# Stick-breaking attention in a two-layer decoder trunk: sigmoids and one reverse running product in place of the log-space chain, the mask added on TensorE, the short query block first, and the four heads as one pipeline

## The reference

```
def stick_breaking_attention(q, k, v):
    """o_t = sum_{s<t} beta_ts prod_{s<j<t}(1-beta_tj) v_s, beta_ts = sigmoid(q_t.k_s/sqrt(d)).
    q, k, v: (B, L, H, Dh)."""
    ...
    def block(start):
        qb = lax.dynamic_slice_in_dim(q, start, Q_BLOCK, axis=1)
        z = jnp.einsum("bqhd,bkhd->bhqk", qb, k, preferred_element_type=jnp.float32) * scale
        causal = key_pos[None, :] < (start + jnp.arange(Q_BLOCK))[:, None]
        log_1m = jnp.where(causal, jax.nn.log_sigmoid(-z), 0.0)
        csum = jnp.cumsum(log_1m, axis=-1)
        log_w = jax.nn.log_sigmoid(z) + (csum[..., -1:] - csum)
        w = jnp.where(causal, jnp.exp(log_w), 0.0)
        return jnp.einsum("bhqk,bkhd->bqhd", w.astype(v.dtype), v)
```

## Time and profile before

| | us |
|---|---|
| median of three executions | 3452.55 |
| lowest and highest | 3443.03, 3460.74 |
| span of the profiled execution | 3441.6 |
| PE busy, weight loads busy | 2945.9 (86%), 2782.7 (81%) |
| DVE busy | 1343.9 (39%) |
| POOL busy | 944.0 (27%) |
| ACT busy | 746.9 (22%) |
| mean granted TensorE clock | 0.922 of full speed |

### The profile page before, as it was taken

How to read it: one execution, slowest core, us unless ns; L and a number is a source line. 1 busy time by engine, 2 the same in 40 slices (tenths; PEclk the granted TensorE clock), 3 DMA queues, 4 the chain that set the end, 5 groups by cost and what they waited for, 6 DMA issues and landing times.

```text
span 3441.6 us, 45325 instructions
## 1 busy us (share of the span) xinstructions
PE 2945.9 (86%) x17797; PEld 2782.7 (81%) x17797; DVE 1343.9 (39%) x2281; ACT 746.9 (22%) x1270; POOL 944.0 (27%) x390
## 2 busy tenths in 40 slices
PE   3999978776668899999999987755997999999996
PEld 2999966664448799999999986645996999999995
DVE  2664055544571544443434234063025332233223
ACT  3321133434562320000000033112033000000002
POOL 2344200000003333333434330400531544354430
PEclk8999988987778999999999998877998999999998
DMA  4222510000102211111122213686111211111101
GB/s 154 75 98 92 114 44 25 25 25 19 37 19 70 87 57 63 63 63 63 66 71 85 87 46 75 139 193 158 62 58 58 83 49 49 37 49 49 49 25 66
DMA packets 175482, 236.23 MB, mean 69 GB/s; under 512 B 56480, under 2 KB 140960, under 8 KB 173088
## 3 DMA queue, kind: packets, MB, share of 16 engines
q1 hardware_dynamic: 66064, 133.42, 13.0%
q10 hardware_dynamic: 109328, 101.54, 9.8%
HBM read 172.37 MB, written 62.55 MB: 68 GB/s over the span
## 4 chain that ended last, share of the span: by engine, by line
issue 34%; PE 32%; POOL 11%; DVE 9%; DMA 6%; ACT 5%; ACTq 2%; SPq 1%; POOLq 0%; DVEq 0%
POOL w_hi L554 7%; PE psum L582 7%; PE psum L583 6%; PE psum L584 6%; POOL w_lo L558 3%; DMA stage<-wstream 3%; PE psum L636 3%; DVE area L1701 2%; PE psum L825 2%; PE psum L817 1%; DVE area L2036 1%; PE psum L936 1%; DVE area L1706 1%; DMA area<-xT 1%; PE psum L833 1%
## 5 line engine op out<-in xcount | busy, mean ns | idle before, releaser
L582 PE MATMUL psum<-x_hi,w_hi 128*128 128x344 f32 (+2 forms) x3600 | 1176.8, 327 | 56.9 <-DVE x_lo L1724 34.3
L583 PE MATMUL psum<-x_lo,w_hi 128*128 128x344 f32 (+2 forms) x3600 | 1170.1, 325 | 0.0
L584 PE MATMUL psum<-x_hi,w_lo 128*128 128x344 f32 (+2 forms) x3600 | 1165.3, 324 | 0.0
L554 POOL TENSOR_TENSOR w_hi<-stage,const 128x1024 fp32r<-128x1024 f32 x193 | 471.8, 2445 | 2386.9 <-PE psum L584 2365.6
L582 PEld LDWEIGHTS psum<-x_hi,w_hi 128*128 128x128 f32 x3600 | 690.8, 192 | 62.3 <-DVE x_lo L1724 32.7
L583 PEld LDWEIGHTS psum<-x_lo,w_hi 128*128 128x128 f32 x3600 | 689.8, 192 | 1.9
L584 PEld LDWEIGHTS psum<-x_hi,w_lo 128*128 128x128 f32 x3600 | 690.8, 192 | 0.0
L558 POOL TENSOR_TENSOR w_lo<-stage,w_hi 128x1024 fp32r<-128x1024 f32 x193 | 475.8, 2465 | 15.1
L582 PE MATMUL psum<-act_hi,w_hi 128*128 128x344 f32 (+1 forms) x1056 | 347.8, 329 | 36.9 <-DVE area L2081 29.3
L2068 DVE TENSOR_TENSOR area<-area,psum 128x352 f32<-128x352 f32 (+1 forms) x132 | 68.0, 515 | 723.7 <-ACT area L1475 723.7
L584 PE MATMUL psum<-act_hi,w_lo 128*128 128x344 f32 (+1 forms) x1056 | 342.1, 324 | 0.0
(11 more groups left out here) (214 smaller groups left out, 2571.8 us busy)
## 6 DMA issues: line engine op xcount, KB each, us to landing
stage<-wstream SPq DMA_DIRECT2D x193, 512.0 KB, 3.3
s_set<-area ACTq DMA_DIRECT2D x8, 1860.0 KB, 7.0
proj<-area ACTq DMA_DIRECT2D x28, 520.0 KB, 2.7
area<-proj ACTq DMA_DIRECT2D x40, 256.0 KB, 4.4
resid<-area ACTq DMA_DIRECT2D x6, 1376.0 KB, 6.0
area<-resid ACTq DMA_DIRECT2D x6, 1376.0 KB, 8.3
area<-proj ACTq DMA_DIRECT2D x12, 520.0 KB, 4.6
area<-xT ACTq DMA_DIRECT2D x4, 1376.0 KB, 8.3
```

What stands on the lines that cost most here:

```text
L554: pool.tensor_tensor(per_block(w_hi[:, slot, :]), per_block(stage[:, h, :]), all_ones, ALU.mult).then_inc(high_split, 1)
L582: mm(out[:, 0:n], w_hi[:, slot, wk], hi[:, xk, a:a + n], start=first, stop=False)
L583: mm(out[:, 0:n], w_hi[:, slot, wk], lo[:, xk, a:a + n], start=False, stop=False)
L584: return mm(out[:, 0:n], w_lo[:, slot, wk], hi[:, xk, a:a + n], start=False, stop=last)
```

## The change

The weight of a key is now sigmoid(z) times the product of sigmoid(-z) over the nearer keys. Per block ACT makes two sigmoids straight from the scores' banks (`sb_gates`), DVE one reverse running product and one multiplication (`sb_weights`). The mask is a second product on TensorE: the identity times a tile `neg` that holds -1e30 above and on the diagonal is added to the scores of the block's own keys, so that sigmoid(z) is 0 there and sigmoid(-z) is 1. The short query block (16 rows) comes first, so that block i > 0 sees 16 + 128 i keys. g counts the blocks of all four heads, and one unrolled pipeline of 36 steps runs over them; q, k, v, the transposed values and the turned weights have two buffers each. The loads of the first two heads are issued ahead of the last DeltaNet block's work on ACT, and a table set with the sigmoid is loaded after it.

```
 def sb_views(carve):
...
+    v = {"wt": [carve(BLOCKS * P * i, BLOCKS, P) for i in range(2)]}
+    at = 2 * BLOCKS * P
+    v["beta"] = [carve(at + T * i, T) for i in range(3)]
+    v["stay"] = [carve(at + T * (3 + i), T) for i in range(2)]
...
+    v["neg"] = carve(at + 2 * BLOCKS * P, P)
...
+            def sb_scores(g):
+
+                hd, i = divmod(g, BLOCKS)
+                q0, nq, nk = query_block(i)
...
+                if g > 1:
+                    pe.wait_ge(sk["beta"], g if i in (0, BLOCKS - 1) else g - 1)
                 for a in range(0, nk, 512):
                     m = min(512, nk - a)
...
+                    z = bank[2 * (i % 2) + a // 512]
+                    d = max(q0, a)
+                    last = mm(z[0:nq, 0:m], sv["q"][hd % 2][:, q0:q0 + nq], sv["k"][hd % 2][:, a:a + m],
+                              start=True, stop=d >= a + m)
+                    if d < a + m:
+                        last = mm(z[0:nq, d - a:m], ident[:, 0:nq], sv["neg"][:, d - q0:a + m - q0], start=False, stop=True)
                 last.then_inc(sk["z"], 1)
...
+            for g in range(HEADS * BLOCKS):
+                sb_turn(g)
+                if g + 2 < HEADS * BLOCKS:
+                    sb_scores(g + 2)
+                sb_out(g)
+                if g % BLOCKS == V_AT and g // BLOCKS < HEADS - 1:
+                    sb_values(g // BLOCKS + 1)
...
             act.wait_ge(dn["qkv_loaded1"], 48 * 5)
             act.wait_ge(dn["z_loaded1"], 16 * 5)
...
+            act.wait_ge(dn["out"], BLOCKS - 1 + 2)
+            load_head(0)
+            load_head(1)
+            dn_act_blocks(BLOCKS - 1, (BLOCKS - 1) // 2, 1, TAIL)
+
+
+            nc.scalar.preload_act_table_set("sigmoid_and_others")
             act.wait_ge(dn["out"], BLOCKS + 2)
...
+            def sb_gates(g):
+
+                i = g % BLOCKS
+                _, nq, nk = query_block(i)
+                z = psum[0:nq, 2 * (i % 2):2 * (i % 2) + (nk + 511) // 512, :].rearrange("p b c -> p (b c)")[:, 0:nk]
+                act.wait_ge(sk["z"], g + 1)
+                if g > 1:
+                    act.wait_ge(sk["w"], g - 1)
+                A(sv["stay"][g % 2][0:nq, 0:nk], z, ACT.Sigmoid, scale=-1.0).then_inc(sk["stay"], 1)
+                if g > 2:
+                    act.wait_ge(sk["w_t"], turn_group(g - 3) + HEAD_GROUPS[(g - 3) % BLOCKS])
+                A(sv["beta"][g % 3][0:nq, 0:nk], z, ACT.Sigmoid).then_inc(sk["beta"], 1)
...
+            for g in range(HEADS * BLOCKS):
+                sb_evac(g)
+                if g + 2 < HEADS * BLOCKS:
+                    sb_gates(g + 2)
+                    if (g + 2) % BLOCKS == BLOCKS - 1 and g // BLOCKS < HEADS - 2:
+                        load_head(g // BLOCKS + 2)
+                sb_high(g)
+                if g % BLOCKS == V_AT and g // BLOCKS < HEADS - 1:
+                    sb_value_evac(g // BLOCKS + 1)
...
+            def sb_weights(g):
+
+                _, nq, nk = query_block(g % BLOCKS)
+                stay, beta = sv["stay"][g % 2], sv["beta"][g % 3]
+                rev = stay[0:nq, nk - 1::-1] if nk == T else stay[0:nq, 0:nk][:, ::-1]
+                dve.wait_ge(sk["stay"], g + 1)
+                ch(V.tensor_tensor_scan(rev, rev, rev, 1.0, mul, ALU.min))
+                ch.sync()
+                dve.wait_ge(sk["beta"], g + 1)
+                V.tensor_tensor(beta[0:nq, 0:nk - 1], beta[0:nq, 0:nk - 1], stay[0:nq, 1:nk], mul).then_inc(sk["w"], 1)
...
+            sb_weights(0)
+            sb_weights(1)
+            for g in range(HEADS * BLOCKS):
+                if g + 2 < HEADS * BLOCKS:
+                    sb_weights(g + 2)
+                sb_low(g)
```

More of the change, by code:

```diff
@@ L101, with query_block, value_group, turn_group @@
 GROUPS_BEFORE = {"gates": 0, "in_proj": 6, "w_out_a": 90, "w_out_b": 96, "ssm_in": 114, "glu_a": 138, "glu_b": 150}
-WT_BEFORE = [sum((i + 4) // 4 for i in range(b)) for b in range(BLOCKS)]
-WT_GROUPS = 3 + sum((i + 4) // 4 for i in range(BLOCKS))
+def query_block(i):
+    q0 = TAIL + (i - 1) * P if i else 0
+    return q0, P if i else TAIL, q0 + (P if i else TAIL)
+V_AT = 4
+HEAD_GROUPS = [(i + 4) // 4 for i in range(BLOCKS)]
+def value_group(hd):
+    return 0 if hd == 0 else hd * 3 + (hd - 1) * sum(HEAD_GROUPS) + sum(HEAD_GROUPS[0:V_AT + 1])
+def turn_group(g):
+    hd, i = divmod(g, BLOCKS)
+    return 3 + hd * (3 + sum(HEAD_GROUPS)) + sum(HEAD_GROUPS[0:i]) + (3 if i > V_AT and hd < HEADS - 1 else 0)
 GATE_DVE = 3
@@ new lines, in sb_scores, with sb_turn @@
+                last.then_inc(sk["z"], 1)
+            def sb_turn(g):
+                _, nq, nk = query_block(g % BLOCKS)
+                pe.wait_ge(sk["w"], g + 1)
+                for n, j0 in enumerate(range(0, g % BLOCKS + 1, 4)):
+                    t = turn_group(g) + n
+                    pe.wait_ge(sk["wt_sb"], t - 1)
+                    for j in range(j0, min(j0 + 4, g % BLOCKS + 1)):
+                        w = min(P, nk - j * P)
+                        last = pe.transpose(bank[4 + t % 2][0:w, j % 4 * P:j % 4 * P + nq],
+                                            sv["beta"][g % 3][0:nq, j * P:j * P + w], ident[0:nq, 0:nq])
+                    last.then_inc(sk["w_t"], 1)
@@ new lines, in sb_evac @@
+            def sb_evac(g):
+                i = g % BLOCKS
+                nq = query_block(i)[1]
+                if g > 1:
+                    act.wait_ge(sk["o"], g - 1)
+                for n, j0 in enumerate(range(0, i + 1, 4)):
+                    t = turn_group(g) + n
+                    nj = min(4, i + 1 - j0)
+                    k = slice(0, TAIL) if j0 == i else slice(0, P)
+                    act.wait_ge(sk["w_t"], t + 1)
+                    A(sv["wt"][g % 2][k, j0:j0 + nj, 0:nq],
+                      bank[4 + t % 2][k, 0:nj * P].rearrange("p (j q) -> p j q", j=nj)[:, :, 0:nq], ACT.Copy
+                      ).then_inc(sk["wt_sb"], 1)
@@ new lines, in sb_high @@
+            def sb_high(g):
+                q0, nq, _ = query_block(g % BLOCKS)
+                act.wait_ge(sk["o"], g + 1)
+                A(x_hi[:, HEADS + g // BLOCKS, q0:q0 + nq], bank[6 + g % 2][:, 0:nq], ACT.Copy).then_inc(sk["o_hi"], 1)
+            sb_value_evac(0)
+            sb_gates(0)
+            sb_gates(1)
+            for g in range(HEADS * BLOCKS):
[7 more added lines that the diff above has]
+                    sb_value_evac(g // BLOCKS + 1)
```

214 lines of the change are left out of this document (52 added, 162 removed).

## The result

The changed kernel takes 3343.79 us in the median of four executions (3331.69 to 3347.99), the kernel before 3448.45 beside it (3443.03 to 3460.74). The medians are 104.7 us apart. The ratio of the executions is 0.9685 [0.9657, 0.9712], with its 95% interval. Forecast were 3356 and 96.2 us less.

A forecast was written before the change was run, and what follows sets the result against it. The prediction took hand-overs in a circle to bound the heads, with no engine full, and PE to bound them afterwards. Savings of 95.6 + 6.5 - 3.4 - 5.0 + 2.5 = 96.2 us off 3452.55 gave 3356, range 3336 to 3390.

The forecast's parts named there:

- The forecast's case: Whole kernel: PE bounds the heads at full clock, 96.2 us saved, 3356 us; chance 0.74.
- The work left on PE: Heads' stage: scores, outputs, turns and masks take PE 30.8 us a head at full clock.
- The bound moves to PE: Heads' stage: PE becomes the likely bound, 30.8 us a head against 20.1 on DVE and 22.4 on ACT.
- Scans by product at the adding scan's price: DVE in the heads: a product scan costs no more than an adding one, 0.157 us and 2.084 ns a key.
- The stage's sum: Heads' stage: PE's 123.2 us plus waits, load issues, start, drain and half-clock steps make 137.9 against 233.5, 95.6 saved.
- The loads' wait: Ahead of the heads: the idle wait for the first head's loads goes, 6.5 us saved.
- The last DeltaNet block starts later: Last DeltaNet block: its squares wait for the previous block's low part and six load issues, 3.4 us lost.
- The table loads: Output projection's norms: eight added table loads, 10.3 us in all, half taken as lost, 5.0 us.
- The warm projection: Output projection's start: PE comes warm from the heads instead of at half clock, 2.5 us saved.
- The falling clock: Rival, heads' stage: PE's clock keeps falling, stage 168 us, 30 more, kernel 3386 us; chance 0.14.
- No overlap: Rival, heads' stage: the pipeline does not overlap, 282 us for four heads, kernel about 3503 us, slower; chance 0.01.
- half clock throughout: Rival, heads' stage: PE stays at half clock, 231 us in place of 138, kernel 3449 us, no change; chance 0.03.

The follow-up runs named there:

- loads_late: The changed kernel with the first two heads' loads issued behind the last DeltaNet block instead of ahead of it: 3340.59 us, ratio 0.9697 to the kernel before.
- ln_set_back: The changed kernel with the logarithm and exp table set loaded once behind the last head: 3330.8 us; projection's start to third norm's low part 174.4 us, not 177.8.
- short_last: The changed kernel with the 16-query block last instead of first in each head: 3333.47 us, heads' stage 126.6 us against 132.9.
- changed_again: The changed kernel run again with no edit, beside the other kernels: 3346.3 us, heads' stage 133.3 us.
- two_masks: The changed kernel with every mask product on PE made twice: 3359.21 us, heads' stage 140.2 us against 132.9.
- dve_one: The changed kernel with one more unread DVE multiplication per block over the block's keys: 3337.33 us, heads' stage 130.8 us against 132.9.
- loads_behind_squares: The changed kernel with the first two heads' loads issued right behind the last DeltaNet block's squares instead of ahead: 3331.45 us, ratio 0.9653 to the kernel before.
- the two long-chain kernels: The changed kernel with the old chain's passes and hand-overs put back on ACT and DVE, heads joined or separate: 3572.5 and 3589.91 us.

## Why the prediction was right

The forecast's case came in, 12 us below its figure and well inside the range.

- **The work left on PE** was forecast as 30.8 us a head, with 20.1 on DVE and 22.4 on ACT. A warm head has 30.59, 19.45 and 19.15 by its window, which counts overlapping instructions once. The groups of the stage, which count each in full, sum to 80.6 on DVE and 86.6 on ACT, 20.2 and 21.7 a head.
- **The bound moves to PE.** Shown from both sides: 2.07 us for 11 products of PE, nothing for 10.5 us of DVE.
- **Scans by product at the adding scan's price**: 2324 ns for 1040 keys by 2.084 a key and 0.157 gives 2324.
- **The stage's sum** was 137.9 and came to 132.9. A head with its waits was to be 31.8 and is 32.05. Two terms were too large. The load issues behind a head's last gates, 2.7, cost nothing: the second head carries them and takes 32.05 like the third, which has none. Start, drain and the first steps at half clock, 3.0 and 5.0, were together 132.9 - 4 x 32.05 = 4.7. The mask product was sized at 0.256 us by the outputs and costs 0.19.
- **The loads' wait**, 6.5: exactly (6.8 to 0.3), and back with loads_late.
- **The last DeltaNet block starts later**: forecast 3.4, measured 5.3. The step held its issues (3.0) and missed the load wait that was moved with them (2.3). I read the moved lines as waits already met.
- **The table loads**: 5.0 forecast, 3.4 to 3.6 measured. **The warm projection**: 2.5 forecast, 2.5 measured (first norm's first copy 6.65 us after the projection's start before, 4.19 after). Together they were to lose 2.5 us; the stretch to the third norm gained 2.1 (179.9 to 177.8), by the 3 us that ln_set_back leaves unexplained.
- **The falling clock** was the chief rival, and did not come in the changed kernel: PE was at 0.50 for the first 8 us while it was full, at 0.98 in the next four, and at 1.00 in heads two to four. The Trainium skill, page TensorE: Matmul & The Clock Gate, Part 1, has sustained activity release the clock; these rows agree. "No overlap" and "half clock throughout" fell with the same rows. In short_last the clock did fall to 0.50 once inside the stage, for 6.4 us, so the margin is small.
- **The span and the median.** I took the saving off a median 10.95 above the profiled span. The executions' own times stand 1.8 us above their spans (3347.99 and 3346.2), so the 10.95 was the spread of three executions, of which the profiled one was most likely the lowest, 1.4 us above its span. The change in the median is larger than that in the spans (104.7 against 95.4) for the same reason, and for one from the other side: the profiled execution of the changed kernel is the slowest of its four, and 10.1 us of it are the last DeltaNet block at a clock of 0.57. In changed_again that block takes 59.8 us with the same code.
- **The sum came out close partly by luck.** The spans differ by 95.4, next to 96.2, but the parts do not match as well: the heads gave 5.0 more than forecast, the norms 4.6 more and the rest of the program 1.9, which nothing forecast; against that the slow last DeltaNet block cost 10.1, which no term held, and its later start about 2 more than its term.

What I had not asked is whether each part of the edit earns its place. The short block first costs 2.0 us a head and the joint pipeline gives 0.7 a boundary. What is left over for nearly all of the gain is the shorter chain, the order of DVE's work and the higher clock beside a full PE; no run of its own shows it. How the 100.6 us divide between fewer passes, the order, the added buffers and the clock stays open, since the two long-chain kernels changed the lead as well.

## What to carry to other kernels

Where no engine is full and the clock is low, look for the circle of hand-overs, add up how long one round of it takes and count how many blocks it yields. Once the fullest engine is covered, its own work is the time, and here an estimate from its rows was good to 1% (30.8 and 30.59 us a head). Then look at that engine's small pieces: a tile cut so that the small remainder is the stationary side or the contraction, and not the moving side, pays for a full one. When waits are moved with the code, ask of each when the transfer it waits for was issued.

## What the hardware showed that I had not expected

- The same last DeltaNet block took from 59.6 to 74.6 us in the profiled executions, at granted clocks of 0.81 to 0.57: 59.7 in two_masks, 64.5 before, 67.4 in dve_one, 69.7 in loads_behind_squares, 74.6 in the changed kernel. The runs' spread of some 16 us (3331.69 to 3347.99) is of that size.
- The stage's start varied too: the first head took 32.05 us in dve_one, whose clock was at 1.00 four microseconds into the stage, and 34.5 in changed_again, where it was at 0.50 for eight.
- A product of 16 rows of contraction was no cheaper than one of 128: 321 ns against 280 in the mean of the groups above.
